# Encoder block on one Trainium2 core: the feed-forward's plain tile products replaced by a seven-product scheme, with two of its block sums per weight slab on GpSimd

## What is computed

```python
def conv_glu_ffn(h, w_gate, w_up, conv_w, conv_b, w_down):
    gate = h @ w_gate                       # 512x2048 @ 2048x5632
    gate = conv(gate, conv_w, width 3, one filter per column) + conv_b
    return (silu(gate) * (h @ w_up)) @ w_down   # 512x5632 @ 5632x2048
h = h + conv_glu_ffn(rmsnorm(h, norm2_g), ...)
return rmsnorm(h, final_norm_g)
```

## Time and profile before

| what | value |
|---|---|
| runs | 2385.77, 2384.22, 2384.5 us; median 2384.5 |
| profiled execution: its span | 2383.3 us (the page has no other time of its own for it; the runs lie 0.9 to 2.5 us above) |
| TensorE (PE) busy | 2340.9 us, 98% |
| weight loads (PEld) busy | 1916.7 us, 80% |
| VectorE (DVE) busy | 975.3 us, 41% |
| ScalarE (ACT) busy | 719.1 us, 30% |
| GpSimd (POOL) busy | 39.7 us, 2% |
| mean granted TensorE clock | 0.997 |
| HBM read, written | 217.37 MB, 4.19 MB |

### The profile page before, as it was taken

How to read it: one execution, slowest core, us unless ns; L and a number is a source line. 1 busy time by engine, 2 the same in 40 slices (tenths; PEclk the granted TensorE clock), 3 DMA queues, 4 the chain that set the end, 5 groups by cost and what they waited for, 6 DMA issues and landing times.

```text
span 2383.3 us, 26573 instructions
## 1 busy us (share of the span) xinstructions
PE 2340.9 (98%) x10613; PEld 1916.7 (80%) x10613; DVE 975.3 (41%) x1333; ACT 719.1 (30%) x930; POOL 39.7 (2%) x48
## 2 busy tenths in 40 slices
PE   6999999999999999999999999999999999999997
PEld 5887888887777787888888888888888888888886
DVE  4223444643564436343343434343433434343434
ACT  5224443423343233331222222221312222222214
POOL 1000000000000000000000000000000000000002
PEclk9999999999999999999999999999999999999999
DMA  5332212222242232333333232333333323223233
GB/s 174 98 96 82 62 54 71 63 79 80 80 150 67 75 97 73 114 98 97 97 97 95 94 95 96 96 97 97 97 97 97 97 97 95 94 95 95 96 97 106
DMA packets 113488, 222.43 MB, mean 93 GB/s; under 512 B 6862, under 2 KB 9140, under 8 KB 112788
## 3 DMA queue, kind: packets, MB, share of 16 engines
q1 hardware_dynamic: 111684, 215.07, 29.0%
q0 software_dynamic: 1744, 6.52, 0.8%
HBM read 217.37 MB, written 4.19 MB: 93 GB/s over the span
## 4 chain that ended last, share of the span: by engine, by line
PE 96%; ACT 1%; DVE 1%; DMA 1%; issue 0%; SPq 0%; ACTq 0%; DVEq 0%
PE dense L508 59%; PE side L508 30%; PE side L681 1%; PE side L664 1%; PE side L628 1%; PE side L624 1%; PE side L546 1%; DMA xin<-in_x 1%; PE side L671 1%; PE side L611 1%; PE side L568 0%; PE side L592 0%; PE side L640 0%; ACT L910 0%; PE side L581 0%
## 5 line engine op out<-in xcount | busy, mean ns | idle before, releaser
L1104 DVE TENSOR_TENSOR w_lo<-raw,w_hi 128x1024 fp32r<-128x1024 f32 x388 | 476.7, 1229 | 1068.1 <-ACT w_hi L843 1066.2
L843 ACT ACTIVATE w_hi<-raw 128x1024 fp32r<-128x1024 f32 x388 | 411.4, 1060 | 1241.5 <-PE dense L508 763.4
L508 PE MATMUL dense<-xT_hi,w_hi 128*128 128x512 f32 x1232 | 486.4, 395 | 0.0
L508 PE MATMUL dense<-xT_hi,w_lo 128*128 128x512 f32 x1232 | 480.2, 390 | 0.0
L508 PE MATMUL dense<-xT_lo,w_hi 128*128 128x512 f32 x1232 | 480.2, 390 | 0.0
L508 PE MATMUL side<-xT_hi,w_hi 128*128 128x512 f32 x704 | 273.9, 389 | 0.0
L508 PE MATMUL side<-xT_lo,w_hi 128*128 128x512 f32 x704 | 273.9, 389 | 0.0
L508 PE MATMUL side<-xT_hi,w_lo 128*128 128x512 f32 x704 | 273.9, 389 | 0.0
L508 PEld LDWEIGHTS dense<-xT_hi,w_hi 128*128 128x128 f32 x1232 | 231.8, 188 | 51.7 <-issue 4.8
L508 PEld LDWEIGHTS dense<-xT_hi,w_lo 128*128 128x128 f32 x1232 | 231.6, 188 | 48.8
L508 PEld LDWEIGHTS dense<-xT_lo,w_hi 128*128 128x128 f32 x1232 | 231.9, 188 | 47.6 <-issue 1.2
(11 more groups left out here) (189 smaller groups left out, 2131.4 us busy)
## 6 DMA issues: line engine op xcount, KB each, us to landing
raw<-in_w_in SPq DMA_DIRECT2D x98, 512.0 KB, 3.6
raw<-in_w_gate SPq DMA_DIRECT2D x88, 512.0 KB, 3.5
raw<-in_w_up SPq DMA_DIRECT2D x88, 512.0 KB, 3.5
raw<-in_w_down SPq DMA_DIRECT2D x88, 512.0 KB, 3.7
raw<-in_w_out SPq DMA_DIRECT2D x32, 512.0 KB, 3.7
xin<-in_x SPq DMA_DIRECT2D x4, 1024.0 KB, 9.8
hid<-in_x POOLq DMA_DIRECT2D x4, 1024.0 KB, 11.0
out<-hid SPq DMA_DIRECT2D x8, 512.0 KB, 4.4
```

Of the source, the lines that this page charges most:

```text
L508: mm = pe.matmul(o, lhs, rhs, start=first and k == 0, stop=last and k == 2)
L843: act.activation(w_hi[slot][:, :], raw[slot][:, :], ACT.Copy).then_inc(hi_done, 1)
L1104: dve.tensor_tensor(w_lo[slot][:, :], raw[slot][:, :], w_hi[slot][:, :].bitcast(F32), ALU.subtract)\
```

## The change

The feed-forward is cut in two phases, and all its products go by a Strassen scheme of the kind with 7 products and 15 sums. A weight slab of 256x512 is a 2x2 arrangement of blocks of 128x256 (two row tiles, two column halves); the activations are cut the same way (two row tiles of the inner dimension, two halves of 256 rows). From four weight blocks come seven operands (three of the blocks as loaded, and four sums), from four activation blocks seven as well. A slab is then seven products, each of two 128x128 weight tiles by 256 columns in three fp32r matmuls: 42 matmuls of 256 columns for 24 of 512. Seven PSUM banks hold the seven products of a pass, a pass being 8 slabs (one group's w_gate or w_up) or 5 to 6 slabs (w_down). At a pass's end seven results are combined to four.

- Phase 1: for each of 11 groups, a w_gate pass and a w_up pass. The activation operands (`slot_hi`, `slot_lo`, 8 slots of 128x1792) are made once from the normed input and stay in SBUF. Gated activations and their four sums are made on GpSimd (`gated`, `act_sums`) and stored to DRAM (`act_d`, 2 MB a group). The residual is spilled to DRAM (`hid_d`) beforehand.
- Phase 2: w_down in 4 chunks of 5 or 6 slabs by 4 column blocks, 16 passes. Activation operands come back from DRAM, 22 times 128x1792 (`load_pair`), and are split into hi and lo again (`refill_slot` on ScalarE, `refill_rest` on VectorE). Results go to `res`, part on VectorE and part on GpSimd (`add_res`).
- Per slab: VectorE makes two block sums in one instruction of 512 (`b_sums`), GpSimd the two that depend on them, one after the other, of 256 each (`last_sums`), ScalarE rounds all seven operands (`f_split`, 1792 wide), VectorE subtracts (`f_rest`, 1792 wide). The split was 1024 wide.
- Per pass: ScalarE saves the first bank (`save_u1`), VectorE does seven additions of 512 (`combine`), each with a PSUM operand.
- The hardware loop is gone: the feed-forward is written out, 264 slabs. The final norm is done once for all rows, at the end.

The diff, cut to what the prediction speaks of (all of it is new text; line numbers of the new program are in the order excerpts):

```diff
+HP = 256
+NB = 7
+PAIRS = KT // 2
+SLOTS = 7
+CHUNKS = [range(0, 6), range(6, 12), range(12, 17), range(17, 22)]
+PRODUCTS = ((0, 0), (2, 2), (5, 5), (4, 4), (3, 3), (6, 1), (1, 6))
+FREED = (0, 1, 2, 3, 5, 6, 7)
...
+            def last_sums(f):
+                t = stage[f % RING]
+                pool.wait_ge(t_first, f + 1)
+                pool.tensor_tensor(t[:, 6 * HP:7 * HP], t[:, HP:2 * HP], t[:, 5 * HP:6 * HP], ALU.subtract)\
+                    .then_inc(t_second, 1)
+                pool.wait_ge(t_second, f + 1)
+                pool.tensor_tensor(t[:, 7 * HP:8 * HP], t[:, 6 * HP:7 * HP], t[:, 3 * HP:4 * HP], ALU.subtract)\
+                    .then_inc(t_done, 1)
...
+            for f in range(3):
+                last_sums(f)
+            for f in range(NF):
+                p, i = SLABS[f]
+                what, g, pairs, _ = PASSES[p]
+                if f + 3 < NF:
+                    last_sums(f + 3)
+                if p == 0 and 2 + i < PAIRS:
+                    xsum(2 + i, i)
+                if p and p <= P2 and (what == "gate" or p == P2):
+                    if i < 2:
+                        gated(p // 2 - 1, 2 * i)
+                        gated(p // 2 - 1, 2 * i + 1)
+                    elif i < 4:
+                        act_sums(p // 2 - 1, 2 * i - 4)
+                        act_sums(p // 2 - 1, 2 * i - 3)
+                if p > P2 and i < 2:
+                    add_res(p - 1, 2 * i)
+                    add_res(p - 1, 2 * i + 1)
...
+                pe.wait_ge(f_lo_done, f + 1)
+                if p == 0:
+                    pe.wait_ge(slot_lo_done, k + 1)
+                if what == "down" and PASSES[p][1] == 0:
+                    pe.wait_ge(slot_lo_done, PAIRS + k + 1)
+                for n, (a, b) in enumerate(PRODUCTS):
+                    if first and p:
+                        if n == 0:
+                            pe.wait_ge(u1_done, p)
+                        else:
+                            pe.wait_ge(comb_done, NB * (p - 1) + FREED[n])
+                    elif first and n == 2:
+                        pe.wait_ge(xs_filled, 6)
+                    for m in range(2):
+                        part = slice(m * P, (m + 1) * P)
+                        o = acc[n][:, m * HP:(m + 1) * HP]
+                        xh, xl = half(slot_hi[slot][:, :], HP)[:, a], half(slot_lo[slot][:, :], HP)[:, a]
+                        wh, wl = half(f_hi[ring][:, :], HP)[:, b], half(f_lo[ring][:, :], HP)[:, b]
+                        if what == "down":
+                            trio = ((xh[:, part], wh), (xl[:, part], wh), (xh[:, part], wl))
+                        else:
+                            trio = ((wh[:, part], xh), (wh[:, part], xl), (wl[:, part], xh))
+                        for z, (lhs, rhs) in enumerate(trio):
+                            mm = pe.matmul(o, lhs, rhs, start=first and m == 0 and z == 0, stop=last and z == 2,
+                                           skip_group_check=True)
+                    if n == NB - 1:
+                        mm.then_inc(f_slab, 1)
+                    elif last:
+                        mm.then_inc(product_done, 1)
...
+            def f_split(f):
+                ring = f % RING
+                act.wait_ge(t_done, f + 1)
+                if f >= RING:
+                    act.wait_ge(f_slab, f - RING + 1)
+                act.activation(f_hi[ring][:, :], stage[ring][:, HP:], ACT.Copy).then_inc(f_hi_done, 1)
...
+            def b_sums(f):
+                ring = f % RING
+                t = stage[ring]
+                dve.wait_ge(stage_in[ring], 16 * (f // RING + 1))
+                dve.tensor_tensor(half(t[:, 4 * HP:6 * HP], HP), t[:, 0:HP].unsqueeze(1).to_broadcast([P, 2, HP]),
+                                  half(t[:, HP:3 * HP], HP), ALU.subtract).then_inc(t_first, 1)
+            def f_rest(f):
+                ring = f % RING
+                dve.wait_ge(f_hi_done, f + 1)
+                dve.tensor_tensor(f_lo[ring][:, :], stage[ring][:, HP:], f_hi[ring][:, :].bitcast(F32), ALU.subtract)\
+                    .then_inc(f_lo_done, 1)
...
+                c11, c12, c21, c22 = (corner(comb, late, right) for late, right in ((1, 1), (1, 0), (0, 1), (0, 0)))
+                if what == "gate" and g:
+                    dve.wait_ge(act_stored, 32 * g)
+                if what == "up":
+                    dve.wait_ge(conv2, G * (g + 1))
+                dve.wait_ge(u1_done, p + 1)
+                summed(dve.tensor_tensor(c11, U1, bank(1), ALU.add))
+                summed(dve.tensor_tensor(U2, U1, bank(2), ALU.add))
+                x3 = bank(3)
+                dve.wait_ge(comb_done, done + 2)
+                summed(dve.tensor_tensor(c21, U2, x3, ALU.add))
+                summed(dve.tensor_tensor(c12, U2, bank(4), ALU.add))
+                dve.wait_ge(comb_done, done + 3)
+                summed(dve.tensor_tensor(c22, c21, bank(4), ALU.add))
+                x5 = bank(5)
+                dve.wait_ge(comb_done, done + 4)
+                summed(dve.tensor_tensor(c12, c12, x5, ALU.add))
+                x6 = bank(6)
+                dve.wait_ge(comb_done, done + 5)
+                summed(dve.tensor_tensor(c21, c21, x6, ALU.subtract))
...
+                if f + 3 < NF:
+                    b_sums(f + 3)
+                if i == len(pairs) - 1:
+                    combine(p)
+                if f + 2 < NF:
+                    f_rest(f + 2)
+                if p == 0 and 2 + i < PAIRS:
+                    slot_rest(2 + i)
+                if what == "up" and 1 <= i < 1 + G:
+                    taps(g, i - 1)
+                for q in REFILL.get(f, ()):
+                    refill_rest(q)
...
```

More of the change, by code:

```diff
@@ L79, with passes, refills @@
 FF0 = WA0 + HALF * (D // BLK)
-GROUP = 2 * NSL + 2 * (D // BLK)
 RING = 3
+HP = 256
[5 more added lines that the diff above has]
+FREED = (0, 1, 2, 3, 5, 6, 7)
+def passes():
+    out, f = [], 0
+    for g in range(NG):
+        for what in ("gate", "up"):
+            out.append((what, g, range(PAIRS), f))
+            f += PAIRS
+    for c in CHUNKS:
+        for j in range(D // BLK):
+            out.append(("down", j, c, f))
+            f += len(c)
+    return out
+PASSES = passes()
+SLABS = [(p, i) for p, (_, _, pairs, _) in enumerate(PASSES) for i in range(len(pairs))]
+NF = len(SLABS)
+P2 = 2 * NG
+LASTP = len(PASSES) - 1
+def refills():
+    last = {k: (P2 - 1) * PAIRS + k for k in range(SLOTS)}
+    freed, at = {}, {}
+    for p, (what, j, pairs, f) in enumerate(PASSES):
+        if what == "down" and j == 0:
+            for i, q in enumerate(pairs):
+                freed[q] = last[q % SLOTS]
+                at.setdefault(min(freed[q] + 3, f + i - 4), []).append(q)
+        if what == "down" and j == D // BLK - 1:
+            for i, q in enumerate(pairs):
+                last[q % SLOTS] = f + i
+    return freed, at
+FREE_AT, REFILL = refills()
 START = {name: IN0 + NSL * b for b, (name, _, _) in enumerate(IN_BLOCKS)}
@@ L377, in ksplit, with half @@
         def ksplit(t, n):
             return t.rearrange("p (k c) -> p k c", c=n)
[L380 to L398 removed]
+        def half(t, n):
+            return t.rearrange("p (m c) -> p m c", c=n)
@@ new lines, in add_res @@
+            def add_res(p, k):
+                j = PASSES[p][1]
+                done, u, late, right = ((1, u1, 1, 1), (5, u3, 0, 0), (6, u2, 1, 0), (7, u3, 0, 1))[k]
+                t = corner_t(res[j], late, right)
+                pool.wait_ge(comb_done, NB * p + done)
+                if k == 0:
+                    pool.wait_ge(u1_done, p + 1)
+                pool.tensor_tensor(t, t, half(u[:, :], HP), ALU.add).then_inc(res_added, 1)
+            for f in range(3):
+                last_sums(f)
@@ L826, in _ @@
+            for f in range(NF):
+                strassen_slab(f)
         @block.scalar
@@ L1286, in _ @@
             for n in range(FF0):
-                if n:
+                if n and n + 2 < FF0:
                     split(n + 2, n + 2)
+                if n == FF0 - 2:
+                    b_sums(0)
+                    f_rest(0)
+                    b_sums(1)
+                if n == FF0 - 1:
+                    f_rest(1)
+                    b_sums(2)
                 b, i = divmod(n - WG0, HALF)
```

709 lines of the change are left out of this document (372 added, 337 removed).

## The result

The changed kernel takes 2441.1 us (median of 4 runs, 2441.0 to 2442.2) against 2385.1 for the one before (2384.2 to 2385.8, same chip): ratio 1.0237, 95% interval 1.0223 to 1.0250. It is 2.4% slower; 0.5% was forecast, with 2308 to 2465 as the range (2340 to 2440 for the prediction's own case, which the time is just above). The profiled execution spans 2440.4 us, 45.9 over the 2394.5 of the sum.

A forecast was written before the change was run, and what follows sets the result against it. TensorE, 98% busy, bounded the kernel; after the change the VectorE-GpSimd shared path was to bind too. Span 925.5 + 918 + 17 + 511 + 23 = 2394.5 us, median 2396 against 2384.5, 0.5% slower; range 2308 to 2465.

The forecast's parts named there:

- the prediction's own case: Whole kernel: VectorE and GpSimd share a path that binds beside TensorE; 2396 us, range 2340 to 2440, chance 0.58.
- TensorE's part: Feed-forward matmuls: 120.1 ns each at 256 columns, 5.04 us a slab, 105 us less if nothing else limits.
- rival 3: TensorE's weight loads not hidden at 256 columns: 135 ns a matmul, 5.67 us a slab, 2458 us; chance 0.08.
- The lock: VectorE instructions with two SBUF inputs and GpSimd's add up: GpSimd's 512-wide costs VectorE 1.15 us, 256-wide about 0.55.
- Start: Before the first product: norm's factor at 916.0, then scalings, sums, split and rest; TensorE begins at 925.5 for 923.1.
- First pass: First pass of phase 1, making activation operands: six slabs at about 8.2 us for 5.2, with two scalings 17 us extra.
- Phase 1: 11 groups of 16 slabs: shared path 80.0 us against TensorE's 80.7, with handoffs 83.5 a group, 918 us.
- hide a delay of up to about 6 us: Phase 1: three staging buffers cover about 6 us, enough for a combine of 4.4 us but not a lasting deficit.
- Rival 2: VectorE's order: small sums wait behind the rest, 6.0 us a slab in w_gate passes and phase 2; 2480 us, chance 0.17.
- Phase 2: w_down, 88 slabs in 16 passes: shared path 487 us against TensorE's 444, with 5% handoffs 511 us.
- Costs nothing by itself: Moving 2 MB a group to DRAM and 20 MB back is free; without slack, up to 3 us, ten times.
- The end: After the last matmul: additions, norm and all 4 MB of stores, 23 us for 11.3 before.

The follow-up runs named there:

- experiment 3: Changed kernel with only GpSimd's wide instructions (gating, activation sums, residual additions) moved to VectorE, small sums left on GpSimd: 2361.3 us.
- experiment 1: Changed kernel with both small block sums of each slab moved from GpSimd to VectorE, nothing else: 2396.9 us.
- experiment 5: Changed kernel with VectorE's rest cut from 1792 to 256 wide, a probe that leaves six of seven low parts out of the result: 2315.2 us.
- experiment 9: Changed kernel with GpSimd's wide instructions left on GpSimd but issued further apart: 2498.0 us.
- version 8: Changed kernel with wide instructions and the first 11 slabs' block sums on VectorE, residual loads and last activation store issued one at a time: 2331.2 us.

## Why the prediction was right or wrong

- **TensorE's part: right.** 120.0 ns between starts for 120.1; rival 3 (135) is out. The fixed part of 13.4 ns holds at 256, 384 and 512 columns.
- **Prices: right.** 2.01 for 2.04, 0.72 for 0.70, ScalarE's split 1.70 for 1.70, combine 0.68. The estimate of 0.77 us for a small sum and 35 us more, from the 4497 ns of the Trainium skill (GPSIMD Engine Reference, "Elementwise — side-by-side cycle accounting"), was high: the run shows 0.72 to 0.74 undisturbed, nearer the line through the rows.
- **The lock: right, and stronger than told.** The Trainium skill (SBUF — State Buffer, "SBUF: two separate sides") has it hold in both directions. The trace of before showed one; now GpSimd's sum of 0.72 us takes up to 2.54 behind VectorE's rest.
- **Start: +4.8.** The norm's factor came at 917.93 for 915.82; the term took it from the row of before, though the first slabs' sums and rests now stand on VectorE ahead of the last residual additions. The other 2.7 lie in the steps behind it.
- **First pass: the step that was mis-sized, +15.** "GpSimd four of 0.70 + 0.04" left out the block sums ahead of them in the same queue, and that VectorE holds off one of the six for 1.7 us. 10.8 to 12.2 us a turn, for 8.2. With the block sums off that queue the pass took 52.0, under the 59 forecast. The 17 us of the term don't follow from its text either: six slabs at 8.2 for 5.2 are 18 before any scaling.
- **Phase 1: the step that failed is the average, +21.** The sum of 80.0 for the shared path against 80.7 for TensorE was made over a group, and 3% for handoffs laid on top. Handoffs cost nothing (80.6 where the wide ones are gone), and the wide instructions are not 9.2 us in 16 slabs but in four, where the turn is 6.13: 4 x 1.09 = 4.4 us behind TensorE. The sentence "hide a delay of up to about 6 us" took each delay one at a time. Lag, the store's delay of a load and combine's 4.4 us come after each other, and what is over the slack shows, 7.8 us in the slab after combine. The text had named this: a load behind a store costs "up to 3 us, ten times" once the cover is gone. It put nothing in the sum for it, and the measured delays past 3.5 us are 2.1 to 3.8 us, ten times. 5.0 us a group for a forecast of 2.8.
- **Rival 2: its chain is real, its condition was wrong.** It was to start from a lag and to last for all w_gate slabs. The trace shows it beside the wide instructions alone; in plain slabs the small sums stand still just as long and nobody waits.
- **Phase 2: +6**, within the 5% laid on, and in part by luck. The forecast had the shared path longer than TensorE in every slab, over 5.5 us apart. In fact half of the slabs are under 5.2 us apart, and the loss is bunched: 42.0 and 43.8 us for TensorE's 30.2 in the first passes of the first two chunks, 30.2 to 31.3 in their last two. Moving the wide additions took off 33 us (experiment 3), moving the small sums 20 (experiment 1; both together 31), and 7 were a wait for a load behind 4 MB. "Costs nothing by itself" held for phase 1's transfers only while the loads had their lead (experiments 3 and 5), and not at this place, where the text had allowed up to 3 us.
- **TensorE's clock: no term, and not the groups' loss.** The mean granted clock was 1.00 over 1004 to 1902 us, 0.82 over 930 to 1004 (the first pass) and 0.97 over 1902 to 2418 (phase 2). In the first pass and in phase 2 a part of the loss can be slower matmuls after waits; no run tells how much.
- **The end: 22.1 for 23.** Right.

In sum: TensorE was to gain 105 us, and the kernel is 56 slower, so 161 us went elsewhere. 110 of them come off with the same arithmetic and the same engines, by where the sums of 11 slabs, the wide instructions and five transfers stand (2441.1 to 2331.2, which is 2.3% faster than the kernel before).

What stays open: whether the 6.13-us turn is long by the amount of work on the shared path or by its order and the standing still, since experiments 3, 5 and 9 change both; how the groups' loss divides between lag and store, since no run has the one without the other; and the 31 us that phase 2 of version 8 still has over TensorE's 444. Of these some 23 lie in the first pass of each chunk (38.1 and 36.3 us for 30.2, 31.4 and 28.1 for 25.2), where the operands come back from DRAM and are split again. No run moved those; in experiment 5, with the same transfers and refills and only the rest short, these passes take TensorE's own 30.2 and 25.2, so the transfers alone are not the reason.

## What to carry to other kernels

Do not average work that is bunched: write down the slab with the most in it, and what comes right behind it, and ask whether the buffers cover both together. A transfer that is hidden because the loads are issued early is hidden no more when a lag has used up that lead. On two engines that hold each other off, it paid here to place the wide instructions with the long ones on the same engine; what is short could stay across. And before an instruction is moved later, find who waits for it: a store's wait in the queue of the loads cost more here (10 us a group) than the chain that the move was meant to shorten (5).

## What was not expected of the hardware

- VectorE and GpSimd, both with work queued, take turns one instruction at a time: in experiment 1 four wide ones took 7.58 us (1.9 each for 1.30 alone) while VectorE's 0.42 us became 1.40. One turn of VectorE's four took 7.7 us (1365.34 to 1373.03) for 3.55 of its own and about 4 x 1.1 of GpSimd's: the sum of both, so next to nothing ran beside the other.
- In the first pass TensorE worked and waited in turn: its first four slabs came 10 to 13 us apart, and over 929 to 981 us it was busy 37.0 of 52. There the granted clock went between its two levels, 2.4 and 1.2 GHz; in experiment 1, with the same four slabs 7 to 9 us apart, it was back at 2.4 before 943 and stayed there for the rest of the pass. Windows of the changed kernel and of experiment 1, the same columns as above:

```profile
943.00:957.00 14.00, 11.65 (x74) 11.48 (x73) 7.99 (x9) 6.35 (x6) 7.52 (x8) 0.75 0.13 37
```
```profile
943.00:957.00 14.00, 11.64 (x96) 11.32 (x97) 13.86 (x14) 7.24 (x8) 10.79 (x8) 1.00 0.26 76
```

  At a mean of 0.75 (1.2 GHz for half of the stretch, 2.4 for the rest) the same 11.6 us of busy time hold 74 matmuls, at 1.00 they hold 96. So busy time hid part of the loss: here a late operand cost the wait, and then slower matmuls for a while.
